# Weights by transfers of two ring units instead of one

## The reference

```python
def first_block(x, ...):
    hn = _rmsnorm(h, norm1_g);  proj = hn @ w_in          # 2048 x 4096
    attn_out = _dilated_attention_mixer(q, k, v, cos, sin)
    ssm_out = _s5_mixer(u, ...)                           # scan, gelu, gate y @ w_glu
    h = h + concat([attn_out, ssm_out]) @ w_out
    hn = _rmsnorm(h, norm2_g)
    h = h + (silu(hn @ w_gate) * (hn @ w_up)) @ w_down    # width 5632
    return _rmsnorm(h, final_g)

def hybrid_layer(x, mem, ...):                            # the second block
    h = rmsnorm(x, norm_mix_pre);  proj = h @ w_in        # xr, gr, q, k, v, qm, gates
    # conv + two RG-LRU directions, local attention, attention to mem
    merged = sum(sigmoid(gate_n) * (y_n @ w_br_n))        # three branches
    x = x + rmsnorm(merged @ w_out, norm_mix_post)
    u = square(relu(rmsnorm(x, norm_mlp_pre) @ w_up));  return x + rmsnorm(u @ w_down, norm_mlp_post)
```

## Time and profile before

| | |
|---|---|
| median of 3 runs | 3333.32 us (3332.8 to 3333.52) |
| the profiled execution: its own time | 3332.64 us |
| the profiled execution: span from first to last instruction | 3330.9 us |
| PE busy | 3253.2 us, 98% of the span |
| DVE, ACT, POOL busy | 63%, 47%, 13% |
| weights issued by SP | 1104 transfers, 256 to 512 KB each |
| median from issue to landing, 512 KB | 3.3 to 4.9 us by stage |
| SP's queue | 51.8% of the 16 DMA engines' span |

### The profile page before, as it was taken

One profiled execution on the slowest core, in us unless ns is written; L12 is line 12 of the kernel. 1 busy time (PEld: TensorE's weight loads), 2 busy tenths in 40 slices (PEclk: granted clock), 3 DMA queues, 4 the chain that ended last, 5 costly groups with the idle time before them and its releaser, 6 DMA issues.

```text
span 3330.9 us, 62940 instructions
## 1 busy us (share of the span) xinstructions
PE 3253.2 (98%) x24420; PEld 3112.3 (93%) x24420; DVE 2095.2 (63%) x2403; ACT 1550.1 (47%) x1934; POOL 431.3 (13%) x420
## 2 busy tenths in 40 slices
PE   6999999999999999999999999999999999999998
PEld 6898889999999999999999999999998989999897
DVE  7788887755555545766875666555555655555555
ACT  4444445555334345336773455544344433334343
POOL 3443343300000000512450000000000000000000
PEclk8999999999999999999999999999999999999999
DMA  6444444555555555455555544555555455656554
GB/s 225 151 156 146 153 144 146 184 185 186 177 183 183 173 182 180 148 196 175 171 186 183 170 148 149 177 170 193 185 182 185 151 191 188 189 189 184 191 183 156
DMA packets 169908, 582.68 MB, mean 175 GB/s; under 512 B 19169, under 2 KB 20961, under 8 KB 169505
## 3 DMA queue, kind: packets, MB, share of 16 engines
q1 hardware_dynamic: 160848, 558.16, 51.8%
q0 software_dynamic: 3696, 12.85, 1.2%
q10 hardware_dynamic: 5216, 9.64, 0.8%
HBM read 573.23 MB, written 7.34 MB: 174 GB/s over the span
## 4 chain that ended last, share of the span: by engine, by line
PE 88%; DVE 8%; issue 2%; ACT 2%; ACTq 0%; DVEq 0%; DMA 0%; SPq 0%
PE gemm_psum L370 22%; PE gemm_psum L371 22%; PE gemm_psum L372 22%; PE gemm_psum L342 4%; PE gemm_psum L340 4%; PE gemm_psum L341 4%; DVE weights_lo L1249 3%; PE gemm_psum L364 1%; PE gemm_psum L365 1%; PE gemm_psum L366 1%; ACT weights_hi L763 1%; PE bank_b L382 1%; DVE projections L1537 0%; PE bank_s L615 0%; PE bank_b L636 0%
## 5 line engine op out<-in xcount | busy, mean ns | idle before, releaser
L1249 DVE TENSOR_TENSOR weights_lo<-weights,weights_hi 128x1024 fp32r<-128x1024 f32 (+2 forms) x1104 | 1339.9, 1226 | 970.4 <-ACT weights_hi L763 965.1
L763 ACT ACTIVATE weights_hi<-weights 128x1024 fp32r<-128x1024 f32 (+2 forms) x1104 | 1109.6, 1018 | 1359.7 <-PE gemm_psum L372 971.9
L370 PE MATMUL gemm_psum<-x_hi,weights_hi 128*128 128x256 f32 x4864 | 1391.9, 286 | 32.3 <-DVE weights_lo L1249 32.2
L371 PE MATMUL gemm_psum<-x_lo,weights_hi 128*128 128x256 f32 x4864 | 1380.9, 284 | 0.0
L372 PE MATMUL gemm_psum<-x_hi,weights_lo 128*128 128x256 f32 x4864 | 1380.6, 284 | 0.0
L370 PEld LDWEIGHTS gemm_psum<-x_hi,weights_hi 128*128 128x128 f32 x4864 | 938.0, 193 | 43.2 <-issue 22.8
L371 PEld LDWEIGHTS gemm_psum<-x_lo,weights_hi 128*128 128x128 f32 x4864 | 938.1, 193 | 1.0
L372 PEld LDWEIGHTS gemm_psum<-x_hi,weights_lo 128*128 128x128 f32 x4864 | 937.9, 193 | 0.0
L370 PE MATMUL gemm_psum<-u_hi,weights_hi 128*128 128x256 f32 x1856 | 535.4, 288 | 17.6 <-DVE weights_lo L1249 15.2
L372 PE MATMUL gemm_psum<-u_hi,weights_lo 128*128 128x256 f32 x1856 | 525.7, 283 | 0.0
L371 PE MATMUL gemm_psum<-u_lo,weights_hi 128*128 128x256 f32 x1856 | 525.7, 283 | 0.0
(11 more groups left out here) (378 smaller groups left out, 2912.4 us busy)
## 6 DMA issues: line engine op xcount, KB each, us to landing
weights<-in_w_branch SPq DMA_DIRECT2D x192, 512.0 KB, 3.3
weights<-in_w_gu SPq DMA_DIRECT2D x176, 512.0 KB, 3.4
weights<-in_w_up SPq DMA_DIRECT2D x128, 512.0 KB, 3.4
weights<-in_w_down SPq DMA_DIRECT2D x128, 512.0 KB, 3.4
weights<-in_w_dn SPq DMA_DIRECT2D x64, 512.0 KB, 3.5
weights<-in_w_in_qk SPq DMA_DIRECT2D x32, 512.0 KB, 3.3
weights<-in_w_mem_k SPq DMA_DIRECT2D x32, 512.0 KB, 3.4
weights<-in_w_mem_v SPq DMA_DIRECT2D x32, 512.0 KB, 3.6
```

Source lines behind the costliest of these rows:

```text
L370: pe.matmul(o, wh, xh[:, kk, :], start=first, stop=False)
L371: pe.matmul(o, wh, xl[:, kk, :], start=False, stop=False)
L763: act.activation(HI[:, j % RING, 0:g.kt * GC], RAW[:, j % RING, 0:g.kt * GC], ACT.Copy)\
L1249: dve.tensor_tensor(LO[:, j % RING, cols], RAW[:, j % RING, cols], HI[:, j % RING, cols].bitcast(f32), ALU.subtract).then_inc(lo_done, 1)
```

## The change

SP moves two units by one transfer. Where a body had eight transfers it has four, of units (0,1), (2,3), (4,5) and (6,7). A transfer goes to two neighbouring slots of the ring, so it waits until both are free, and the four semaphores of the slots become two, one for a pair. ACT waits for the pair's semaphore ahead of either unit. With kt = 4 a transfer is 1 MB, with kt = 3 it is 768 KB and with kt = 2 it is 512 KB. Nothing else is changed: ACT, DVE and PE have the same instructions in the same order.

```diff
-        raw_in = [sem(f"raw_in{n}") for n in range(RING)]
+        raw_in = [sem(f"raw_in{n}") for n in range(RING // 2)]
...
                         if g is in_u and b() == 0 and j < 4:
                             sp.dma_start(H[:, 4 * j:4 * j + 4, :], A["x"][:, 4 * j:4 * j + 4, :]).then_inc(x_in[j], 16)
-                        wait(sp, lo_done, b(SLOTS, SLOTS * g.first + j - RING + 1))
-                        sp.dma_start(RAW[:, j % RING:j % RING + 1, 0:g.kt * GC],
-                                     g.w[ix(b(2, j // UNITS)), j % UNITS].rearrange("a p n -> p a n"))\
-                          .then_inc(raw_in[j % RING], 16)
+                        if j % 2 == 0:
+                            wait(sp, lo_done, b(SLOTS, SLOTS * g.first + j + 1 - RING + 1))
+                            sp.dma_start(RAW[:, j % RING:j % RING + 2, 0:g.kt * GC],
+                                         g.w[ix(b(2, j // UNITS)), j % UNITS:j % UNITS + 2].rearrange("a u p n -> p (a u) n"))\
+                              .then_inc(raw_in[j % RING // 2], 16)
...
             def upper(g, b, j):
-                wait(act, raw_in[j % RING], b(32, 32 * g.first + 16 * (j // RING) + 16))
+                wait(act, raw_in[j % RING // 2], b(32, 32 * g.first + 16 * (j // RING) + 16))
```

## The result

The changed kernel takes 3390.82 us (median of four runs, 3387.77 to 3394.86), the kernel before, run beside it on the same chip, 3333.42 (3332.8 to 3334.41). The ratio is 1.0173, with a 95% interval of 1.0155 to 1.0190: slower. The profiled execution took 3389.22 us with a span of 3387.5, so 56.6 us more than the one before. The prediction was 3379, with a range of 3357 to 3404.

The account below looks back on a forecast made before the run. PE was taken as the bound (matmuls in its pipeline 3253.2 of 3330.9 us), its longest waits being for DVE's splits. Terms summed to +46.0 us on the profiled 3332.6, so 3379, range 3357 to 3404.

Parts of the forecast that it names:

- Stages where PE is the bound: Some 950 of 1104 units: cost 0, since unit 508's timeline leaves 6.0 us for a landing of 4.45.
- The fourth split: Last of DVE's four-split group now waits for a load released by the first: glu +8, out_ssm +14.2, dn2 +14.6.
- L: Landing time of a two-unit transfer after issue: 3.2, 3.95 and 4.45 us for units of 256, 384 and 512 KB.
- H: ACT's upper part and hand-over after landing: 0.67, 0.88 and 1.10 us for units of 256, 384 and 512 KB.
- out_attn: Stage whose small units are nearly late at a few places: an estimate of +1 us.
- Start: ACT's first upper part needs both first units, which land at 9.8 instead of 8.5: +0.9 us.
- lru_in: Late loads of unit 482, +2.4 us, and unit 486, +2.0; low clock behind the last wait, at 487, +1.7.
- The clock inside the cycles: Low-clock stretches expected in out_ssm and dn2, hidden within each cycle because PE's work is shorter: cost 0.
- rival 1: Slower by the clock: PE stays at the low level in out_ssm and dn2, +67 us, 3446 at most; chance 0.07.
- Rival 2: Slower by the landing: L at its upper end adds 2.0 us at 22 links, +44, 3423; chance 0.10.
- Rivals 3: No change or less: the second unit's load hides, 3333 to 3338 us; chance 0.05.
- 4: Faster by fewer and larger transfers, ACT's waits for weights go: 3328 us at best; chance 0.04.

Follow-up runs that it names:

- experiment 1: Kernel before, but the even unit's transfer also waits for the odd unit's slot; each unit keeps its own transfer: 3363.38 us, ratio 1.0089.
- experiment 2: Kernel before with that late release, single transfers, and ACT takes an even unit only when the odd one has landed: 3389.69 us, ratio 1.0170.
- experiment 6: Changed kernel with other pairs: units (1,2), (3,4), (5,6) of each eight together, 7 and 0 alone, RAW slots moved by one: 3353.21 us, ratio 1.0061.
- 7: Changed kernel with pairs (4k+1, 4k+2) only, in all stages, 4k and 4k+3 alone, slots as they were: 3338.94 us, ratio 1.0016.
- experiment 4: Changed kernel with pairs only in stages whose units are smaller than 512 KB, single transfers elsewhere: 3383.25 us, ratio 1.0149.
- experiment 9: Kernel before, single transfers, with matmul events two units behind the splits instead of three in glu, out_ssm and dn2: 3363.55 us, ratio 1.0088.
- experiment 5: Changed kernel with pairs only in 512 KB-unit stages, without in_u, first gate-and-up stage and lru_in: 3333.45 us, ratio 1.0000.

## Why the prediction was right, and by how much it was off

The cost is where it was put and of the kind it was said to be, within 12 us of 57. By its steps:

- Stages where PE is the bound, cost 0: right. From lru_gate on the difference grows by 0.0, and the run with pairs in such stages alone is at 1.0000. Where PE runs undisturbed, the 6.0 us read at unit 508 held: after the change it is issued at 1550.73, lands at 1555.79 and is taken at 1556.88. But they didn't hold throughout. ACT waited up to 4.9 us at once for in_w_up, and there it was the next cover named, the lead of the splits over PE, that hid it: unit 860 is issued at 2681.39 and taken at 2687.64, 2.2 us late, its split ends at 2690.0, and PE gets to it at 2693.5.
- The fourth split: right as a mechanism (experiments 1 and 2 rebuild the loss from its two parts; the pairs of 6 and 7 take it away again in out_ssm and dn2). **The step that was mis-sized is L**: 3.2, 3.95 and 4.45 us in the sum, 3.5, 4.4 and 5.0 by the medians of the transfers that a fourth unit waits for, and 5.2 for unit 482. That is 12 x 0.3 = 3.6 us of the 6.1 missing in glu and out_ssm and 7 x 0.45 = 3.2 of the 4.0 missing in dn2. With the time from landing to the fourth split, also a little longer than H, the distances are 0.41 and 0.55 above the forecast, which makes 12 x 0.41 + 7 x 0.55 = 8.8 of these 10.1 us. In the rest of the program the misses nearly cancel: out_attn 2.2 too low, gu0 to gu2 1.8 too high. I took the second unit's time from two transfers in a full queue and the first's from one issued alone; in experiment 2 the second of two single transfers lands 3.2 us behind the issue of the first, and one transfer of the same bytes (3.5) 0.3 later still.
- The estimate for L by the Trainium skill, 3.2, 3.8 and 4.4 us ("DMA: Bandwidth & Descriptors", section "Anatomy of one DMA — SWDGE (gpsimd) path"), is short in the same way; these transfers are issued by SP, and the traces decide: 3.5, 4.4, 5.0.
- out_attn was an estimate of +1 and is +3.2. It has pairs of 512 KB, +0.5 by the late release alone (experiment 1), and +3.2 with pairs (experiment 4).
- Start: +0.9 predicted; no cost is to be seen. ACT's first upper part starts at 8.79, not at 9.8 (8.90 before):

```profile
6.91 1.70 ACT L784 ACTIVATE x_hi<-residual,vecs 128x256 fp32r<-128x256 f32 x4
8.79 1.06 ACT L764 ACTIVATE weights_hi<-weights 128x1024 fp32r<-128x1024 f32 x1 [0.17 <-DMA weights<-in_w_in_u]
```

  The x piece came first this time and ACT worked on it while the 1 MB landed. The +0.8 up to mem_v can't be put down to the change: it is in_u's -1.0 and in_qk's +1.5, and both are also there with single transfers (experiment 9; experiment 1 has the first alone).
- lru_in: 6.1 predicted, 6.0 measured, but not of the parts I gave. Unit 482's distance grew from 3.30 to 6.46 (1472.90 to 1479.36), +3.2 and not +2.4; unit 486's showed as +0.4 and not +2.0; the clock took the rest, about 2.4. It was low behind PE's wait for unit 483, the one after the late 482, rather than behind that for 487:

```profile
1486.20:1492.80 6.60, 5.36 (x25) 5.39 (x26) 4.44 (x3) 0.78 (x2) 4.30 (x6) 0.50 0.61 218
```

- The clock inside the cycles, cost 0: right (9.30 and 9.23 us, above), and rival 1 with it falls. The rule named ahead, that a PE which waits in each round starts it at the low clock, is the Trainium skill's ("TensorE: Matmul & The Clock Gate", section "HAM oscillation — how this bites in real kernels"): the trace agrees in part, since PE waits in each of the six cycles named above, and three have a clock of 0.82 and three of 0.97 to 1.00.
- Rival 2 (3423) had L twice as long: the time went a quarter of the way from the forecast to it. Rivals 3 and 4 fall by experiments 1 and 5.

## What to carry to other kernels

In a ring of buffers, look at what releases a slot before looking at how many bytes a transfer has: a transfer of two units waits for the later of two releases and is awaited by the earlier of two uses. Where that release is a step of the same burst that needs the load, a whole landing comes into the burst, and each round pays it; where the release is in the burst before, the same pair costs nearly nothing (+6 us with half of the bytes in pairs, against +57). This has to be looked at in every stage: another pairing that freed out_ssm and dn2 lost 16 us in stages that the change had left alone (experiment 6). Where a load was already covered, larger transfers neither gained nor lost here (experiment 5).

## What the runs showed that I had not expected

- Time from issue to landing, medians of whole stages: 512 KB 3.3 (3.7 to 3.9 as a pair of 256 KB units), 768 KB 4.4, 1 MB 5.0, 1.5 MB 6.4, 2 MB 7.8 us. From 1 MB to 2 MB it is 1.4 us per 512 KB, from 512 KB to 1 MB 1.7; two queued transfers at the start of the kernel landed 1.27 apart.
- Single transfers issued two at a time take longer by the median too: 512 KB in in_w_branch 4.0 us in experiment 1 and 4.3 in experiment 2, 3.3 in the kernel before.
- Sums of ACT's waits for weights say little. The run that is as fast as before has 71.9 us of them for in_w_up alone, and the kernel before shows none over 6.6 us.
- What a low stretch of the clock costs depends on what the loop is made of: at most 0.1 us a cycle in one, 1.3 in another, for stretches of about the same 3.4 us.
